# Inverse roots of the norms: square root on ScalarE and reciprocal on VectorE in place of logarithm and exponential

## What is computed

```python
def rms_norm(x, g):
    y = x * lax.rsqrt(jnp.mean(x * x, axis=-1, keepdims=True) + 1e-6)
    return y * g

h = rms_norm(x, norm_mix[i]) * (1.0 + sc1) + sh1      # before each mixer
x = x + g1 * mix
h = rms_norm(x, norm_ffn[i]) * (1.0 + sc2) + sh2      # before each feed-forward network
k = rms_norm(lat, k_gain)                             # keys of layer 1
attn = rms_norm(attn, attn_out_g)                     # layer 2, attention half
rec = rms_norm(rec, hgrn_out_g) * silu(g_h)           # layer 2, recurrence half, by head
```

## Time and profile before

| | |
|---|---|
| time, median of 3 runs | 1092.78 us (1092.67 to 1094.19) |
| the profiled execution's own time | 1092.73 us |
| its span, first to last instruction | 1091.0 us |
| PE busy | 1069.7 us, 98% |
| DVE busy | 808.4 us, 74% |
| ACT busy | 337.6 us, 31% |
| granted TensorE clock, mean | 0.997 of full |
| table loads on ACT | 55, of 1283 ns each |

### The profile page before, as it was taken

How to read it: one execution, slowest core, us unless ns; L and a number is a source line. 1 busy time by engine, 2 the same in 40 slices (tenths; PEclk the granted TensorE clock), 3 DMA queues, 4 the chain that set the end, 5 groups by cost and what they waited for, 6 DMA issues and landing times.

```text
span 1091.0 us, 18364 instructions
## 1 busy us (share of the span) xinstructions
PE 1069.7 (98%) x7516; PEld 972.7 (89%) x7516; DVE 808.4 (74%) x1392; ACT 337.6 (31%) x799; POOL 23.9 (2%) x83
## 2 busy tenths in 40 slices
PE   6999999999999999999999999999999999999998
PEld 4788889999999977888899999998898889999997
DVE  2477769888898848544789889887896298887755
ACT  3243324111111245663511111116355342222101
POOL 1000240000000000000000000000000000000000
PEclk9999999999999999999999999999999999999999
DMA  9999936888878662281868878775342255853421
GB/s 343 281 385 340 316 114 251 304 317 281 320 279 295 199 78 77 86 259 53 318 214 322 313 270 309 271 243 162 117 155 78 80 172 170 290 185 107 145 72 39
DMA packets 163013, 234.82 MB, mean 215 GB/s; under 512 B 8770, under 2 KB 137842, under 8 KB 162930
## 3 DMA queue, kind: packets, MB, share of 16 engines
q1 hardware_dynamic: 162428, 233.27, 63.5%
q10 hardware_dynamic: 501, 0.38, 0.1%
HBM read 232.19 MB, written 1.44 MB: 214 GB/s over the span
## 4 chain that ended last, share of the span: by engine, by line
PE 88%; DVE 7%; ACT 2%; issue 1%; DMA 1%; ACTq 1%; DVEq 0%
PE PS L869 34%; PE PS L915 13%; PE PS L799 11%; PE PS L827 6%; PE PS L990 6%; PE PS L812 4%; PE PS L1117 3%; PE PS L791 1%; PE PS L720 1%; PE PS L1475 1%; DVE scratch L2480 1%; PE PS L1321 1%; PE PS L1277 1%; DVE top L2479 1%; PE PS L1070 1%
## 5 line engine op out<-in xcount | busy, mean ns | idle before, releaser
L915 PE MATMUL PS<-act,slots 128*128 128x256 f32 x704 | 159.8, 380 | 0.4 <-DVE act L2191 0.4
L1962 DVE SCALAR_TENSOR_TENSOR ada_acc<-ada_slots,cond,ada_acc 128x1024 f32<-128x1024 f32 x119 | 152.6, 1282 | 5.1 <-DMA ada_slots<-in_ada_w 0.9
L1607 ACT ACTIVATE PS<-PS 128x128 f32<-128x128 f32 x180 | 53.5, 297 | 304.4 <-PE PS L869 304.4
L915 PEld LDWEIGHTS PS<-act,slots 128*128 128x128 f32 x704 | 130.5, 190 | 18.9 <-issue 1.6
L799 PE MATMUL PS<-hT,slots 128*128 128x256 f32 x656 | 144.3, 380 | 0.8 <-ACT hT L1569 0.8
L799 PEld LDWEIGHTS PS<-hT,slots 128*128 128x128 f32 x656 | 123.9, 190 | 19.2 <-issue 3.0
L869 PE MATMUL PS<-hT,slots 128*128 128x128 f32 x960 | 127.0, 275 | 0.0
L869 PE MATMUL PS<-oT,slots 128*128 128x128 f32 x960 | 126.8, 275 | 0.0
L869 PEld LDWEIGHTS PS<-hT,slots 128*128 128x128 f32 x960 | 119.6, 192 | 2.5
L869 PE MATMUL PS<-oT,scratch 128*128 128x128 f32 x960 | 117.1, 275 | 0.0
L869 PEld LDWEIGHTS PS<-oT,slots 128*128 128x128 f32 x960 | 116.8, 192 | 0.0
(11 more groups left out here) (403 smaller groups left out, 1405.4 us busy)
## 6 DMA issues: line engine op xcount, KB each, us to landing
ada_slots<-in_ada_w SPq DMA_DIRECT2D x144, 512.0 KB, 8.5
slots<-in_ffn_w_up SPq DMA_DIRECT2D x44, 1024.0 KB, 11.8
slots<-in_ffn_w_down SPq DMA_DIRECT2D x22, 1024.0 KB, 5.0
slots<-in_w_up SPq DMA_DIRECT2D x22, 1024.0 KB, 5.2
slots<-in_sb_w_in SPq DMA_DIRECT2D x11, 1024.0 KB, 13.1
slots<-in_w_in SPq DMA_DIRECT2D x11, 1024.0 KB, 5.4
slots<-in_dsa_w_in SPq DMA_DIRECT2D x10, 1024.0 KB, 5.3
ada_slots<-in_w_down SPq DMA_DIRECT2D x2, 2816.0 KB, 12.7
```

The costliest lines, as they stand in the source:

```text
L915: last = mm(PS[:, c // 2, (c % 2) * T:(c % 2) * T + T], w[:, j_odd * D + c * P:j_odd * D + (c + 1) * P], act[:, j_odd, :], start=start and ...
L1607: act_e.activation(dst.rearrange("p (x t) -> p x t", x=copies), stem(at).unsqueeze(1).to_broadcast([P, copies, P]), ACT.Copy).then_inc(see ...
L1962: ins = dve.scalar_tensor_tensor(dst, ada_slot[k][:, :], c, dst, ALU.mult, ALU.add)
```

## The change

`Sqrt` takes the place of `Ln`, and `Exp` is gone. DVE takes the reciprocal where it first needs the result. The table of `Sqrt` is loaded at the place where that of `Ln` was; in `norm_raw` the table of `Silu` is loaded right behind the root; for the attention half of layer 2 the table of `Sqrt` is loaded ahead of the squares; and for the last feed-forward network it is still there from the root before.

```diff
             def root(dst, ps):
                 full(2)
-                link(act_e.activation(dst, ps, ACT.Ln, bias=eps_col[:, :]))
-                act_e.activation(dst, dst, ACT.Exp, scale=-0.5).then_inc(unit_read[2], 1)
+                act_e.activation(dst, ps, ACT.Sqrt, bias=eps_col[:, :]).then_inc(unit_read[2], 1)
 
-            def norm_root(bank):
-                act_e.preload_act_table(ACT.Ln)
+            def norm_root(bank, load_table=True):
+                if load_table:
+                    act_e.preload_act_table(ACT.Sqrt)
                 act_e.wait_ge(stat_full, bk("stat_full").next())
-                link(act_e.activation(rstd[:, :], PS[:, bank, 0:T], ACT.Ln, bias=eps_col[:, :]))
-                act_e.activation(rstd[:, :], rstd[:, :], ACT.Exp, scale=-0.5).then_inc(rstd_ready, 1)
+                act_e.activation(rstd[:, :], PS[:, bank, 0:T], ACT.Sqrt, bias=eps_col[:, :]).then_inc(norm_root_ready, 1)
...
             def norm_raw(units, load_table=True):
...
-                norm_root(0)
+                norm_root(0, load_table)
+                act_e.preload_act_table(ACT.Silu)
...
             skip(2)
+            act_e.preload_act_table(ACT.Sqrt)
             act_e.wait_ge(unit_read[2], bk("unit_full2").value())
             act_e.activation(attn_sq[:, :, :], oT[:, 0:4, :], ACT.Square, scale=(AH * 64) ** -0.5).then_inc(attn_squared, 1)
...
-            norm_raw(OUT_UNITS[2])
+            norm_raw(OUT_UNITS[2], load_table=False)
...
+            def inverse_root():
+                dve.wait_ge(norm_root_ready, bk("norm_root_ready").next())
+                link(dve.reciprocal(rstd[:, :], rstd[:, :]))
...
             def norm(which, chunks=range(KC)):
                 if len(chunks) == KC:
-                    dve.wait_ge(rstd_ready, bk("rstd_ready").next())
+                    inverse_root()
...
                     if not odd and both:
-                        dve.wait_ge(rstd_ready, bk("rstd_ready").next())
+                        inverse_root()
...
             norm_parts(4)
+            inverse_root()
             dve.wait_ge(ada_used[KC - 1], 1)
             ins = vector_sum(6, 1)
             link(ins)
             link(dve.scalar_tensor_tensor(gain[:, 0:KC], ...))
-            dve.wait_ge(rstd_ready, bk("rstd_ready").next())
...
                 if n == 4:
                     root()
+                    link(dve.reciprocal(rstd[:, :], rstd[:, :]))
                     dve.scalar_tensor_tensor(kn[:, :], fm[:, 0, :], gqk[:, :], rstd[:, :], ALU.mult, ALU.mult)\
...
             take_scores(4, 1)
             dve.wait_ge(unit_read[2], rstd_taken)
+            link(dve.reciprocal(rstd[:, :], rstd[:, :]))
...
             root()
+            link(dve.reciprocal(sq_flat[:, D:2 * D], sq_flat[:, D:2 * D]))
```

More of the change, by code:

```diff
@@ L278, in build @@
         stat_full = sem("stat_full")
-        rstd_ready = sem("rstd_ready")
+        norm_root_ready = sem("norm_root_ready")
         gain_ready = sem("gain_ready")
@@ L1573, in squares, with norm_raw @@
                 act_e.activation(hT[:, c:c + k, :], xT[:, c:c + k, :], ACT.Square, scale=D ** -0.5).then_inc(sq_ready, 1)
-            def norm_raw(units):
+            def norm_raw(units, load_table=True):
                 act_e.wait_ge(gain_ready, bk("gain_ready").next())
```

## The result

| | before | after |
|---|---|---|
| time, median of 4 runs | 1092.72 us (1092.16 to 1094.19) | 1107.82 us (1107.19 to 1108.47) |
| the profiled execution | 1092.73 us, span 1091.0 | 1107.19 us, span 1105.5 |
| mean granted TensorE clock | 0.997 | 0.994 |

The account below looks back on a forecast made before the run. PE, busy 98% of the span at full clock, was taken to bound the kernel. Terms for each place summed to 7R + Q - 8.30 = +6.2 us on 1092.73, so 1098.9 us; range 1095.5 to 1108.

Parts of the forecast that it names:

- The three places without a cost: Mixers of layers 1 and 2: -0.33 us each; feed-forward of layer 2: nothing, over 4 us of slack.
- the six at which PE starts later: First norm +0.87, layer 1's keys +1.39, feed-forwards 0 and 1 +1.36 together, layer 2's attention half +0.97, recurrence half +2.26 us.
- The price of the reciprocal: DVE's reciprocal at 4.7 ns a column: R = 1.36 us for 128x256, Q = 4.97 us for 128x1024.
- 7R + Q - 8.30: Sum over all places, R and Q being the reciprocal's times for 256 and 1024 columns: +6.2 us.
- The clock: PE was read as running at full clock; the sum has no term for a slower one.
- its 3.5 to 7.9 ns: Reciprocal's price per column within which the forecast holds, 1096 to 1108 us; chance 77%.
- The meeting at feed-forward 0 and 1: DVE's first input_sums meets PE with 0.71 us of slack: +0.68 us in each layer, +1.36 for both.
- both halves of layer 2: Attention half: slack 0.42, +0.97 us; recurrence half: slack 0.31, Q - 2.71 = +2.26 us.
- the cap of 0.4 us at the mixers: Gain at each mixer of layers 1 and 2 can't exceed 0.4 us, since PE's own work ends there.
- the first norm: The reciprocal stands in front of vector_sum and delays PE's first product: R - 0.49 = +0.87 us.
- the turn: Layer 1's keys: the reciprocal lengthens DVE's chain to PE's first turn, R + 0.03 = +1.39 us.
- No idle to absorb a stall: Most of PE's time follows a stall in order; rival, stalls overlapping unseen waits: 1093 to 1095 us, 3%.

Follow-up runs that it names:

- filler_rec: The changed kernel with nine unread products more on TensorE before the wait for mixed_ready in layer 2's recurrence half; 1105.73 us.
- one_set: The kernel before with one table set holding both Ln and Exp loaded ahead of each of the nine roots; 1090.89 us against 1092.78, ratio 0.9985.
- slack_only: The kernel before with Sqrt and reciprocal only at the mixers of layers 1 and 2 and ahead of layer 2's feed-forward; 1093.11 us, ratio 1.0004.
- rec_only: The kernel before with Sqrt and reciprocal only at layer 2's recurrence half (128x1024); 1098.76 us.
- cheap_op: The changed kernel with each of the nine reciprocals replaced by a multiply-add on the same tile; 1092.02 us, ratio 0.9994 to the kernel before.
- rec_half: The changed kernel with the reciprocal of layer 2's recurrence half taken of 512 of 1024 columns; 1101.93 us.
- keys_undone: The changed kernel with only the root of layer 1's keys made by Ln and Exp again, its reciprocal gone; 1104.88 us.

## Why the prediction was right and wrong

- **Where to look: right in the main.** The three places without a cost (feed-forward 2, the two mixers with their +0.1) and the six at which PE starts later are those that were named.
- **The price of the reciprocal: the first step that failed.** "14 ns for three more columns, 4.7 ns a column" was extrapolated over 250 and 1020 columns from two shapes of one and four. The real slope is 6.26 ns. A line through the two long shapes meets one column at 153.6 ns and four at 172.4; measured are 164 and 178. Both short shapes lie above it, but not by the same amount, and these 5 ns, divided by three columns, took a quarter off the slope. The formula 7R + Q - 8.30 with the true values gives +10.5 us: 4.3 us of the miss are this term.
- **The clock: the second step, missing from the sum, and as large.** The prediction said that the clock is full and followed each stall only to the moment at which PE goes on. In the profiled execution half-clock stretches behind the two longest stalls add 1.6 and 2.9 us, 4.5 together. It had even named the two stalls (L1305's wait, `mixed_ready`) as PE's longest. `filler_rec` shows the cause for the second.
- **The range held by luck in part.** The true slope lies inside its 3.5 to 7.9 ns, but that alone gives 1103.3 us. The clock, which wasn't in the sum, brought the time to 1107.82, 0.2 us under the upper end.
- **The meeting at feed-forward 0 and 1: wrong.** The prediction took `input_sums` for the tightest, with 0.71 us of slack, and announced a wait of 0.7 us there. PE waits earlier, at L915 for `act`, 1.1 us (the waits above). These are the product `act` on DVE before, then the same after with PE's product behind it (timeline: start us, us; PE's start before is in the table, 177.05):

```profile
175.97 0.42 DVE L2191 TENSOR_TENSOR act<-ffn_work 128x256 f32<-128x256 f32 x1
```

```profile
177.49 0.42 DVE L2197 TENSOR_TENSOR act<-ffn_work 128x256 f32<-128x256 f32 x1
178.06 3.26 PE L915 MATMUL PS<-act,slots 128*128 128x256 f32 x14 [1.10 <-DVE act L2197]
```

  DVE makes `act` later by R + 0.03, as said (1.52 us, and PE was 0.26 us ahead), and PE by 1.27: 0.51 us of slack and not 0.71. At `input_sums` nothing is left to wait for.
- **PE's starts, read from the chain: 0.16 us late.** In a row of products without a wait each starts 0.22 us behind the last, and 0.16 us before the last one's modelled end. The chain counts a step from that end. So the prediction read 842.22 and 860.45 where PE's products start at 842.06 and 860.28, and gave both halves of layer 2 about 0.17 us of slack too much. For the same reason a listed wait is 0.16 us shorter than what PE loses: the cap of 0.4 us at the mixers was too low, `one_set` won 0.6 at each.
- **Restart: missing, small.** Behind a wait the second product starts 0.29 us after the first (0.32 at the attention half) in place of 0.22. That is 0.07 to 0.10 us for each new stall. The steps of the chain after show it together with the 0.16 (start us, us, what): the first 16 products follow a wait, the second 16 don't.

```profile
178.06 3.69 PE PS L915 x16
...
188.11 3.46 PE PS L915 x16
```

- **The slack itself: right** at the first norm, +1.26 against +1.26, and at the turn, +1.81 against +1.78. The new position of the reciprocal ahead of `vector_sum` costs what was said (chain after, start us, us, what; before, the first step of `vector_sum` waited for PE alone):

```profile
18.88 0.48 ACT rstd L1562
...
19.39 1.76 DVE rstd L2009
21.15 0.02 issue
21.18 0.44 DVE fm L1992
```

- **No idle to absorb a stall: wrong for the first norm.** In `slack_only`, whose first norm is that of the kernel before, PE reaches the ones product 1.9 us earlier than in the profiled execution before. It then waits for DVE's sums of `ada_acc`, which follow transfers, and starts L730 at 37.23 us (waits of PE; before it was 37.37, after 37.10):

```profile
PE PS L730 <- DVE ada_acc L1965: 1.7, 1, 1.7
```

  `rec_only` and `cheap_op`, with as early a start, wait there too, 0.9 and 1.1 us. So an early start is mostly lost at 37 us, and in such an execution most or all of the 1.26 us at the first norm would be hidden behind this wait. That is argued from these waits and not run by itself. The first two rows of the table can't be taken as costs by themselves.
- **The profiled execution before wasn't neutral.** A half-clock stretch of 3.4 us stands in its first 17 us, behind PE's waits for the first transfers; the changed kernel's has none. The windows from 10 to 15 us, before and after:

```profile
10.00:15.00 5.00, 3.07 (x36) 1.66 (x38) 0.46 (x2) 4.22 (x3) 0.00 (x0) 0.81 1.03 416
```

```profile
10.00:15.00 5.00, 3.18 (x51) 1.69 (x53) 0.46 (x2) 4.22 (x3) 0.00 (x0) 1.00 1.03 415
```

  That is the -1.52 us in the first line of the table. It doesn't explain the spread of 2 us among the runs of the kernel before: of the 21 beside `slack_only`, the three with a mean clock of 0.997 took 1092.78 to 1093.67 us, and the two slowest, 1094.42 and 1094.52, had 0.999. The transfers alone move the start: traces without a stretch there reach the ones product between 14.5 us (`rec_half`) and 16.8 us (`keys_undone`).
- **What the miss is made of.** Of the 14.5 us between the two traces 6.2 were forecast. The rest is 4.3 for the price, 4.5 for the clock, some 0.8 for slack read too large and 0.25 for restarts, less the 1.5 of the start.
- **Rule against row.** I set aside a rule of the Trainium skill, ScalarE: Activation LUTs, section Table sets: the hidden batching unit (one set holds exponential and logarithm), because the trace has a load between the two. The load only showed which set was chosen. By that rule the pair needs one load, and `one_set` agrees: no load between them in any of the nine roots. The Trainium skill, VectorE: DVE Perf Modes, section Walkthrough: the 8-slice pipeline in each mode, names a repeat count of 8 for the reciprocal; read as eight cycles at the page's 0.96 GHz it gives an estimate of 8.3 ns a column, above the measured 6.26.

## What to carry to other kernels

Where engines meet with half a microsecond of slack, a step added on the engine that comes last costs nearly its whole length: price the added instruction at its real size before the rest is argued, and never by a slope from shapes whose time is all fixed part. A stall of a few microseconds on TensorE can cost more than its length, so add the restart and a possible half-clock stretch, or keep TensorE busy through it. Read TensorE's slack from the starts of its products, at every meeting of the stage, and look whether a wait further on would have absorbed the stall. And where a load stands between two functions, ask first whether one table set holds both.

## What the runs showed of the hardware

- RECIPROCAL in fp32 on VectorE: 178 ns for 4 columns, 1749 for 256, 3352 for 512, 6554 for 1024; 6.26 ns a column, where a multiply-add from and to the same tile took 291 ns for 256 columns and 694 for 1024 (0.52 ns a column).
- After 3.9 us of idle time TensorE's granted clock was at 1.2 GHz for 6.8 us in two traces (the changed kernel, `keys_undone`) and for 3.4 us in one (`rec_only`); after 2.7 us it was for 3.4 us in two traces of four; after 0.7 us it wasn't, in one trace. With products in the idle time it stayed at 2.4 GHz (`filler_rec`). In the first 20 us, where TensorE waits for transfers up to 3.7 us in every trace, two of the eleven have a stretch of 3.4 us.
- Going on after a wait costs TensorE some 0.24 us beyond the wait that the profile lists: 0.16 us by which a product otherwise starts before the modelled end of the last one, and 0.07 to 0.10 us between the first and the second product.
- One table set serves `Ln` and `Exp`: with it loaded by name, 17 of 55 table loads of 1283 ns went.
